# One run of 448 words for the gates' high and low part in the stage over V

## The reference, cut to what matters

```
u = jnp.take(expert_u, eb, axis=0)
act = jax.nn.gelu(jnp.einsum('tkd,td->tk', u, xb), approximate=False)
v = jnp.take(expert_v, eb, axis=0)
return jnp.einsum('tk,tkd->td', gb * act, v)
```

## Time and profile before

| what | value |
|---|---|
| time, median of 3 runs | 1914.86 us (1913.74 to 1915.00) |
| profiled execution, span from the first to the last instruction | 1912.2 us |
| median less this span | 2.7 us |
| PE busy | 1896.7 us, 99% |
| PE weight loads busy | 1758.9 us, 92% |
| DVE busy | 1383.4 us, 72% |
| ACT busy | 950.5 us, 50% |
| POOL busy | 1390.8 us, 73% |
| HBM traffic | 443 MB read, 234 GB/s over the span |

### The profile page before, as it was taken

One profiled execution on the slowest core, in us unless ns is written; L12 is line 12 of the kernel. 1 busy time (PEld: TensorE's weight loads), 2 busy tenths in 40 slices (PEclk: granted clock), 3 DMA queues, 4 the chain that ended last, 5 costly groups with the idle time before them and its releaser, 6 DMA issues.

```text
span 1912.2 us, 35061 instructions
## 1 busy us (share of the span) xinstructions
PE 1896.7 (99%) x11798; PEld 1758.9 (92%) x11798; DVE 1383.4 (72%) x2585; ACT 950.5 (50%) x1342; POOL 1390.8 (73%) x708
## 2 busy tenths in 40 slices
PE   9999999999999999999999999999999999999997
PEld 7888889888999999999999999999999999999997
DVE  7534684045545777968888888479889889999986
ACT  6453355475544444544444444455555555555555
POOL 3867768887998999998888888976555525666711
PEclk9999999999999999999999999999999999999999
DMA  8544546564655666666666566689999988999984
GB/s 307 186 143 153 199 144 224 193 190 155 218 188 177 207 209 208 210 202 196 194 192 196 189 195 195 200 280 351 333 336 334 333 297 298 337 325 334 328 273 145
DMA packets 128380, 448.29 MB, mean 234 GB/s; under 512 B 16528, under 2 KB 19472, under 8 KB 127632
## 3 DMA queue, kind: packets, MB, share of 16 engines
q1 hardware_dynamic: 102240, 367.29, 58.5%
q0 software_dynamic: 20480, 67.13, 10.0%
q10 hardware_dynamic: 5584, 12.88, 2.0%
HBM read 443.04 MB, written 4.19 MB: 234 GB/s over the span
## 4 chain that ended last, share of the span: by engine, by line
PE 72%; POOL 17%; issue 8%; DMA 1%; DVE 1%; ACT 0%; POOLq 0%; SPq 0%; DVEq 0%; ACTq 0%
PE ps L1885 22%; PE ps L1982 22%; POOL wlo L438 17%; PE ps L1888 12%; PE ps L1985 11%; PE ps L1899 1%; PE ps L1585 1%; PE ps L1587 1%; PE ps L1586 1%; PE ps L1961 1%; DMA raw<-in_w_front 0%; PE ps L1869 0%; DMA big<-in_x_t 0%; PE ps L1963 0%; ACT whi L539 0%
## 5 line engine op out<-in xcount | busy, mean ns | idle before, releaser
L438 POOL TENSOR_TENSOR wlo<-raw,whi 128x1024 fp32r<-128x1024 f32 x436 | 1057.6, 2430 | 207.9 <-ACT whi L539 193.1
L539 ACT ACTIVATE whi<-raw 128x1024 fp32r<-128x1024 f32 x435 | 461.2, 1060 | 633.7 <-PE ps L1888 361.8
L1885 PE MATMUL ps<-x_parts,whi 128*128 128x448 f32 x2048 | 588.9, 369 | 0.0
L1982 PE MATMUL ps<-gate_parts,whi 128*128 128x448 f32 x1992 | 573.6, 369 | 0.0
L734 ACT ACTIVATE whi<-raw 128x1024 fp32r<-128x1024 f32 x256 | 271.7, 1061 | 294.9 <-PE ps L1985 255.8
L1888 PEld LDWEIGHTS ps<-x_parts,wlo 128*128 128x128 f32 x2048 | 384.7, 188 | 31.3
L1985 PEld LDWEIGHTS ps<-gate_parts,wlo 128*128 128x128 f32 x1992 | 374.2, 188 | 30.8
L1888 PE MATMUL ps<-x_parts,wlo 128*128 128x224 f32 x2048 | 386.9, 270 | 0.0
L1985 PE MATMUL ps<-gate_parts,wlo 128*128 128x224 f32 x1992 | 376.0, 270 | 0.0
L1437 DVE TENSOR_TENSOR wlo<-raw,whi 128x1024 fp32r<-128x1024 f32 x248 | 303.9, 1225 | 68.1 <-ACT whi L734 52.1
L1885 PEld LDWEIGHTS ps<-x_parts,whi 128*128 128x128 f32 x2048 | 310.3, 191 | 0.0
(11 more groups left out here) (266 smaller groups left out, 2217.2 us busy)
## 6 DMA issues: line engine op xcount, KB each, us to landing
raw<-in_w_u SPq DMA_DIRECT2D x256, 512.0 KB
raw<-in_w_v SPq DMA_DIRECT2D x256, 512.0 KB
raw<-in_w_front SPq DMA_DIRECT2D x180, 512.0 KB
big<-in_mem ACTq DMA_DIRECT2D x8, 256.0 KB, 5.6
big<-in_mem_t ACTq DMA_DIRECT2D x2, 1024.0 KB, 6.2
big<-in_x ACTq DMA_DIRECT2D x2, 1024.0 KB, 7.3
x_back<-x2t_scratch ACTq DMA_DIRECT2D x2, 896.0 KB
big<-in_x_t SPq DMA_DIRECT2D x3, 512.0 KB, 8.4
```

The costliest lines, as they stand in the source:

```text
L438: nc.gpsimd.tensor_tensor(wlo[:, j % SPL, :], raw[:, j % RAW, :], whi[:, j % SPL, :], ALU.subtract).then_inc(lo_done, 1)
L539: nc.scalar.activation(whi[:, j % SPL, :], raw[:, j % RAW, :], ACT.Copy).then_inc(hi_done, 1)
L1885: nc.tensor.matmul(sums[:, 0:2 * TD], whi[:, s, cols], x_parts[:, :, m, 0:TD], start=m == 0, stop=False, skip_group_check=True)
L1982: nc.tensor.matmul(sums[:, 0:2 * TD], whi[:, s, cols], gate_parts[:, g, :, 0:TD], start=False, stop=False, skip_group_check=True)
```

## The change

gate_parts gets a second view, gate_both, with the 512 words of a slot in one row. The high part lies in words 0 to 223, as before. The low part lies in words 224 to 447, where it was in words 256 to 479. The matmuls that read both parts read 448 words in one run, where their access pattern had two runs of 224 with a pitch of 256. What is computed is the same, in the same order.

```
+        gate_both = gate_parts.rearrange("p a b c -> p a (b c)")
 gated_high:
-                nc.scalar.activation(gate_parts[:, j % SPL, 0, 0:TD], W[:, k0 + j, :], ACT.Copy).then_inc(ghi_done, 1)
+                nc.scalar.activation(gate_both[:, j % SPL, 0:TD], W[:, k0 + j, :], ACT.Copy).then_inc(ghi_done, 1)
 v_step:
-                nc.vector.tensor_tensor(gate_parts[:, j % SPL, 1, 0:TD], W[:, j % NK, :], gate_parts[:, j % SPL, 0, 0:TD],
+                nc.vector.tensor_tensor(gate_both[:, j % SPL, TD:2 * TD], W[:, j % NK, :], gate_both[:, j % SPL, 0:TD],
                                         ALU.subtract).then_inc(glo_done, 1)
 v_block:
-                nc.tensor.matmul(ps[:, c, 0:2 * TD], whi[:, s, cols], gate_parts[:, g, :, 0:TD],
+                nc.tensor.matmul(ps[:, c, 0:2 * TD], whi[:, s, cols], gate_both[:, g, 0:2 * TD],
-                return nc.tensor.matmul(ps[:, c, TD:2 * TD], wlo[:, s, cols], gate_parts[:, g, 0, 0:TD],
+                return nc.tensor.matmul(ps[:, c, TD:2 * TD], wlo[:, s, cols], gate_both[:, g, 0:TD],
 v_piece:
-                        nc.tensor.matmul(sums[:, 0:2 * TD], whi[:, s, cols], gate_parts[:, g, :, 0:TD],
+                        nc.tensor.matmul(sums[:, 0:2 * TD], whi[:, s, cols], gate_both[:, g, 0:2 * TD],
-                        ins = nc.tensor.matmul(sums[:, TD:2 * TD], wlo[:, s, cols], gate_parts[:, g, 0, 0:TD],
+                        ins = nc.tensor.matmul(sums[:, TD:2 * TD], wlo[:, s, cols], gate_both[:, g, 0:TD],
```

## The result

The changed kernel takes 1917.33 us (median of 20 runs, 1915.87 to 1919.54) against 1913.76 us for the kernel before (20 runs, 1912.82 to 1915.59). The ratio is 1.0017, 95% interval 1.0010 to 1.0023: slower, by 3.3 us by the ratio and 3.6 us by the medians. The forecast was 1914.9 us with a range of 1899 to 1920. The time lies in the range and within the 0.2% that was called no change, but it isn't the time of before: there is a small loss that the forecast didn't have. Its most likely cause is the mechanism of rival two at a fifth of its price.

The account below looks back on a forecast made before the run. TensorE's own pace was taken to bound the kernel, other engines hidden in V. All parts of the change summed to zero, added to the three-run median of 1914.86 us: 1914.9 us, range 1899 to 1920.

Parts of the forecast that it names:

- rival two: V's matmuls fall into a slower pace as operand addresses meet weight loads: 8.75 ns each, 17.9 us, 1932.8 us; chance 0.12.
- What bounds V: Stage over V goes at TensorE's own pace, 0.630 us a group, 645 us in all; ACT and DVE are hidden.
- (a): ACT writes the gates' high part to the same 224 words, 373 ns a piece: nothing changes.
- (b): DVE writes the low part 224 words after the high one, not 256; still 443 ns a piece.
- (c): Small matmuls of L1985 and L1963 read the high part alone, one run of 224: nothing changes.
- Part (d): The 2,048 matmuls of L1982 and L1961 in V read 448 words in one run; the break's cost taken as zero.
- Rival one: Moving operand's address generator loses time at each break: 13.7 us faster, 1901.2 us, far end 1888; chance 0.34.
- the step from 512 words to a break of 6.7 ns: From 230 ns for 512 words, one run of 448 would take 203 ns against 210 for two runs; together 13.7 us.
- the row of L1899: One-run 256-word matmuls in U at 125 ns, 0.488 ns a word, dearer than V's 0.469; so no break cost needed.
- The control from U: L1885 in U, runs 4,096 words apart, has V's 0.63 us a group, so the pitch between runs costs nothing.
- the two paces of the 256-word matmuls: One-run 256-word matmuls at 500 and 555 us took 113 and 118 ns; the 5.0 ns scaled to 8.75 for 448 words.
- What was left over for the 448s: With 224s held by weight loads (107 ns), 448s take 208 ns against 203: 5 ns a break, some 10 us.

Follow-up runs that it names:

- c1: Changed kernel with its one run of 448 words starting at word 32 of the slot, low part at 256: 630.0 ns a group, ratio 1.0001 to the kernel before.
- d1: Kernel before, two runs, both parts moved on by 32 words (32 / 288): 633.3 ns a group in V, ratio 1.0016.
- d2: Changed kernel with its one run starting at word 64 (64 / 288): 633.3 ns a group in V, ratio 1.0017.
- c3: Kernel before, two runs, with the low part at word 232: 633.3 ns a group ahead of the fold, 626.7 behind; first ratio 0.9987, over eleven runs 0.9996.
- d3: Changed kernel with its one run starting at word 8 (8 / 232): 633.4 ns a group ahead of the fold, 626.7 behind, ratio 0.9994.
- d4: Changed kernel with 32 unused words between raw buffers and split weights, moving weights and gates together: V 633.4 ns a group, U 630.0, ratio 1.0024.
- e1: Changed kernel with 32 unused words between split weights and everything behind them: V 630.0 ns a group, U 633.4, ratio 1.0047 to the kernel before.
- c4: Against the kernel before, four runs of 112 words with a pitch of 128: 636.7 ns a group ahead of the fold, 630.0 behind, ratio 1.0017.
- e2: 16 unused words behind the split weights, V with two runs, low part at word 232: V 631.1 then 633.4 ns a group, ratio 1.0016.

## Why the prediction was right or wrong

**What bounds V** held: the change showed in the pace of TensorE alone, with no wait added, and 3.4 us follow from 3.33 ns a group by the same multiplication as in the prediction. That the number came so near, 2.4 us, is in part luck: it stood on the median of three runs, 1914.86 us, where twenty have 1913.76. Nothing in the prediction's own sum has the 3.3 ns.

**Parts (a), (b) and (c)**: the writers kept their times (373 ns; 435 ns for DVE's, which had 443), near to what was said. Part (c) was wrong in a small way: the small matmuls, unchanged in code, are started 100.0 ns apart in place of 102.5, and the two together take 213.3 ns in place of 215.0.

**Part (d), the break at zero** held as far as the runs go: with the low part at the same place one run and two have equal paces (before and c1, d1 and d2, c3 and d3), and even four runs reach 630.0 ns in half of V. Rival one, a fixed time lost at each break, is out, and with it the step from 512 words to a break of 6.7 ns. But the row of L1899, which decided for zero, was read from starts rounded to 10 ns. In the whole trace the first L1899 of a pair starts 122.5 ns ahead of the second, and that one 119.2 ns ahead of the next L1885; a piece of U with such a pair takes most often 2,753 ns against 2,520. That is 233 ns for two, 117 each, 0.455 ns a word, and so a little cheaper by the word than the group of V (0.469) and not dearer. So far as zero was right, this row isn't the reason.

**The control from U was misread.** The prediction said that the pitch between the runs costs nothing since 4,096 and 256 have one pace, and held the same against rival two. Both are multiples of 64 words, and 224 is not. A control that differs in size but not in the remainder that counts can't see this cause. That is the step that failed: the change of the address was put at nothing, and it cost 3.33 ns a group. It is also why rival two got only 0.12.

**Rival two** named the mechanism that was at work, the addresses of the moving operand against the loads of weights, with "from word 256 to word 224" as the point that decides. Its price was taken from the two paces of the 256-word matmuls (8.75 ns for a matmul, 17.9 us). The measured price is 3.33 ns for a group, which is 1.7 ns for each matmul of 448 words if it is put on them alone, 3.4 us. It needed more than 1.9 ns to be called slower by over 0.2%, and fell just short: the point 1.0017 is inside "no change", while the end of its interval is outside.

**What was left over for the 448s.** In both kernels two matmuls of 224 words start 100.0 to 102.5 ns apart, and the next matmul of 448 words starts 112.5 to 113.3 ns behind the second, though each has weights of its own. The page "TensorE: Matmul & The Clock Gate", section "LDWEIGHTS (loading the stationary operand)", gives 107 ns by estimate for such a load; the 224s come to 107.5 and 106.7 ns on the mean, near that, but the single distances don't keep to it, and for those the measurement decides. What the prediction worked out from there, that the rest on the 448s holds some 5 ns for the break, came out the other way: without the break the 448s take 210.0 ns each in the changed kernel and 208.5 in c1, where they took 207.5 with it.

**What stays open.** Why the place of the low part against the weights sets the pace isn't known. That it is a meeting of two reads (the moving operand and the load of the next weights) fits d4, c1 and e1, but no run here separates the two reads; it was only argued. Open too is why places 40, 16 and 56, and the four runs of c4, have more than one pace, and what makes the pace change in the middle of an uninterrupted row, as in d3. No kernel had two runs at the places of the changed one (0 / 288 in a slot, which are 0 and 32 in the period). Such a kernel would tell whether two runs lose the 3.33 ns there too. That the number of runs has no part in the loss is likely from the pairs above, but not shown. That the period is 64 words rests on one pair moved by exactly that (after and d2), on the agreement of U in e1 with d1, and on the places in U.

## What to carry to other kernels

Two long runs in the moving operand of a matmul were as fast as one with the low part at the same place, so in this kernel a layout needn't be changed to make one run out of two. When an operand of a loop like this, bound by TensorE, moves in SBUF, steps of half a per cent in its pace in either direction can come of it, even where the instructions are the same, and check the remainder of each part's offset (here in 64 words), not only its size. Differences of 0.1 to 0.3% between two kernels whose buffers lie differently say nothing about the edit until a kernel with shifted buffers has been run beside them.

## What the runs showed of the hardware

- The pace of a group of four fp32r matmuls comes for the most part in steps of 3.33 ns: 626.7, 630.0, 633.3 and 636.7 ns were each held for more than a hundred pieces, 0.5% apart. Only e2 had one between them, 631.1 ns.
- An idle buffer of 32 words between weights and activations made U 3.4 us slower and V 3.2 us faster in one kernel, and the matmuls of the front slower too (253.3 us for 1,300 of them against 249.5 to 250.1).
- One program can have two paces: the same instructions at the same addresses went at 633.3 ns ahead of the fold and at 626.7 behind it, and in another execution at 626.7 throughout. In d3 the pace changed from 626.7 to 633.3 within an uninterrupted row, too. The two traced executions of c3's kernel took 1914.9 and 1910.7 us, and 3.1 us of the difference lie in V. This is most likely where the spread of 1909 to 1915 us of c3 comes from, against 1912.8 to 1916.0 for the kernel before, timed beside it.
